# A two-layer diffusion backbone on one core: the first mixer's projection as three products of split operands, and weight splits ahead of every norm

## The reference, cut to what matters

```
def rmsnorm(x, g):
    x32 = x.astype(F32)
    y = x32 * lax.rsqrt(jnp.mean(x32 * x32, axis=-1, keepdims=True) + EPS)
    return y.astype(x.dtype) * g
def modulate(x, shift, scale):
    return x * (1 + scale) + shift
...
        a_lat = modulate(rmsnorm(h_lat, norm1_g[l]), sh1, sc1)
        a_ctx = modulate(rmsnorm(h_ctx, norm1_g[l]), sh1c, sc1c)
...
    hy_l, q_l, k_l, v_l = split(a_lat @ w_in)
    hy_c, q_c, k_c, v_c = split(a_ctx @ w_in)
```

## Time and profile before

| | us |
|---|---|
| median of 3 runs | 3494.87 |
| lowest and highest run | 3494.84, 3497.16 |
| the profiled execution | 3494.55 |
| its span, first to last instruction | 3492.7 |

### The profile page before, as it was taken

One profiled execution on the slowest core, in us unless ns is written; L12 is line 12 of the kernel. 1 busy time (PEld: TensorE's weight loads), 2 busy tenths in 40 slices (PEclk: granted clock), 3 DMA queues, 4 the chain that ended last, 5 costly groups with the idle time before them and its releaser, 6 DMA issues.

```text
span 3492.7 us, 46282 instructions
## 1 busy us (share of the span) xinstructions
PE 3290.8 (94%) x18808; PEld 2753.9 (79%) x18808; DVE 1976.6 (57%) x3318; ACT 1209.3 (35%) x1846; POOL 20.0 (1%) x41
## 2 busy tenths in 40 slices
PE   7898979999999999999999999898679999999998
PEld 3355548888888888888888887687569999999997
DVE  3125631899765566344444443434857988756665
ACT  1210422333333333333333332424334444444444
POOL 0000000000000000000000000000000000000000
PEclk9998899999999999999999999899799999999999
DMA  5330022555667666665656553222045777788884
GB/s 195 127 126 0 1 91 73 139 144 143 192 215 243 226 212 205 221 224 193 193 193 193 193 193 100 91 79 79 1 134 170 211 226 247 247 271 263 268 265 150
DMA packets 232411, 587.81 MB, mean 168 GB/s; under 512 B 20791, under 2 KB 103816, under 8 KB 228552
## 3 DMA queue, kind: packets, MB, share of 16 engines
q1 hardware_dynamic: 227088, 528.57, 48.2%
q0 software_dynamic: 4208, 53.27, 3.9%
q10 hardware_dynamic: 904, 3.01, 0.3%
HBM read 483.06 MB, written 101.71 MB: 167 GB/s over the span
## 4 chain that ended last, share of the span: by engine, by line
PE 86%; DVE 10%; ACT 2%; issue 1%; DMA 1%; POOL 0%; SPq 0%; ACTq 0%; DVEq 0%; POOLq 0%
PE ps L504 36%; PE ps L790 31%; PE ps L686 7%; PE ps L742 5%; PE ps L704 2%; PE ps L549 1%; DVE w_lo L1545 1%; PE ps L580 1%; DVE arena L1462 1%; PE ps L647 1%; PE ps L573 1%; PE ps L722 1%; DVE arena L1456 1%; PE ps L859 1%; PE ps L655 0%
## 5 line engine op out<-in xcount | busy, mean ns | idle before, releaser
L1545 DVE TENSOR_TENSOR w_lo<-wring,w_hi 128x1024 fp32r<-128x1024 f32 x512 | 626.0, 1223 | 687.0 <-ACT w_hi L1076 685.0
L504 PE MATMUL ps<-a_hi,w_hi 128*128 128x512 f32 (+1 forms) x2048 | 701.7, 343 | 8.5 <-DVE w_lo L1545 4.4
L790 PE MATMUL ps<-act_hi,w_hi 128*128 128x512 f32 (+1 forms) x2048 | 697.6, 341 | 4.4 <-DVE act_lo L1576 4.4
L504 PE MATMUL ps<-a_hi,w_lo 128*128 128x512 f32 (+1 forms) x2048 | 690.3, 337 | 0.0
L504 PE MATMUL ps<-a_lo_q,w_hi 128*128 128x512 f32 (+1 forms) x2048 | 689.6, 337 | 0.0
L790 PE MATMUL ps<-act_lo,w_hi 128*128 128x512 f32 (+1 forms) x2048 | 688.1, 336 | 0.0
L790 PE MATMUL ps<-act_hi,w_lo 128*128 128x512 f32 (+1 forms) x2048 | 687.6, 336 | 0.0
L1076 ACT CAST w_hi<-wring 128x1024 fp32r<-128x1024 f32 x512 | 533.6, 1043 | 226.8 <-PE ps L790 226.8
L504 PEld LDWEIGHTS ps<-a_hi,w_hi 128*128 128x128 f32 x2048 | 389.6, 190 | 60.9 <-issue 11.5
L790 PEld LDWEIGHTS ps<-act_hi,w_hi 128*128 128x128 f32 x2048 | 387.8, 189 | 51.7 <-issue 4.8
L504 PEld LDWEIGHTS ps<-a_hi,w_lo 128*128 128x128 f32 x2048 | 389.6, 190 | 41.6
(11 more groups left out here) (230 smaller groups left out, 3320.5 us busy)
## 6 DMA issues: line engine op xcount, KB each, us to landing
wring<-in_u SPq DMA_DIRECT2D x256, 512.0 KB, 4.1
wring<-in_v SPq DMA_DIRECT2D x256, 512.0 KB, 3.9
gates<-arena POOLq DMA_DIRECT2D x24, 2048.0 KB, 8.4
acts<-arena SPq DMA_DIRECT2D x128, 256.0 KB, 4.6
arena<-acts SPq DMA_DIRECT2D x128, 256.0 KB, 3.4
arena<-gates SPq DMA_DIRECT2D x16, 2048.0 KB, 11.3
late_ring<-in_ada SPq DMA_DIRECT2D x28, 1024.0 KB, 6.2
wring<-in_ada SPq DMA_DIRECT2D x40, 512.0 KB, 6.8
```

What stands on the lines that cost most here:

```text
L504: ins = pe.matmul(o, l, r, start=n == 0, stop=n == len(pairs) - 1, **kw)
L790: ins = pe.matmul(value_sum(l, c), w, x, start=m == 0 and n == 0 and (l == 0 or c % 2 == 0), stop=m == NKEY - 1 and n == 2, skip_group_che ...
L1545: tt(WLO[:, k % 4].rearrange("p k n -> p (k n)"), wring[:, n % RING * TILE:(n % RING + 1) * TILE], WHI[:, k % 4].rearrange("p k n -> p (k ...
```

## The change

The first projection becomes a split product like the others (entry `ab` of `SPLIT`, ring of two; its high activations are in two pieces, `AB_HI`). The values tile comes out transposed like the rest into `VV`, and PE turns it with four transposes behind `rope`. For all four norms, DVE splits the first weight tiles before it takes the norm's sum, `ring` of them instead of `ring - 1`, and interleaves the low parts with the chunks; PE runs the first `ring` tiles chunk by chunk beside each other, one output bank for each. `ada` counts on a semaphore of its own, `rows_used`, `w_used` starts at the output projection, and `key_numbers` on DVE moves behind `attention`, since `AB_HI` covers its place.

```diff
@@ tables
+        AB_HI = [over(f"ab_hi{n}", at, 4 * T)[:, :].rearrange("p (k t) -> p k t", k=4) for n, at in enumerate((31872, 18432))]
+        VV = arena[:, 33920:34432]
+        ab_parts = weight_parts("ab", 20480, 22528, 2)
+        SPLIT = {"ab": (None, N_ABIN, 0, 0, T, 2, ab_parts, A_LO_Q),
@@ SP, load
-                wait(sp, S["w_used"], n - RING + 1)
+                m = n - RING
+                if m >= AT_ABOUT:
+                    sp.wait_ge(S["w_used"], used(m))
+                elif m in AB_TILE:
+                    sp.wait_ge(S["ab_split"], AB_TILE[m] + 1)
+                elif m >= 0:
+                    sp.wait_ge(S["rows_used"], ADA_GROUP[m] + 1)
@@ PE
             def ab_in():
-                pe.wait_ge(S["a_ready"], KD)
+                if ada_leads(0):
+                    ada(FIRST_GROUPS)
+                first_tiles("ab", lambda j: ps[:, j, :], T, lambda j: None)
                 for j in range(N_ABIN):
-                    n = at_abin(j)
-                    if ada_leads(j):
-                        ada(FIRST_GROUPS + j)
-                    wait(pe, S["ab_taken"], j - 3)
...
+                    if j >= 2:
+                        if ada_leads(j):
+                            ada(FIRST_GROUPS + j)
+                        wait(pe, S["ab_taken"], j - 3)
+                        product("ab", j, ps[:, j % 4, :], T)
...
@@ PE, end of rope
+                for t in range(TT):
+                    ins = pe.transpose(ps[:, 6, t * P:(t + 1) * P], VV[:, t * P:(t + 1) * P], ident[:, :])
+                ins.then_inc(S["vt_ready"], 1)
@@ PE
+            def first_tiles(name, o, width, ready):
+
+                n0, _, _, k, _, ring, _, _ = SPLIT[name]
+                for c in range(KD):
+                    pe.wait_ge(S["a_parts_ready"], KD * k + c + 1)
+                    for j in range(ring):
+                        if c == 0:
+                            ready(j)
+                            split_done(name, j)
+                        product_part(name, j, c, o(j), width)
@@ PE, queries; hg_in likewise with two tiles
-                for j in range(N_WQ):
-                    wait(pe, S["wq_taken"], N_WQ * l + j - 3 if j >= 4 else 0)
+                first_tiles(f"wq{l}", lambda j: ps[:, j, 0:width], width, lambda j: None)
+                for j in range(4, N_WQ):
+                    pe.wait_ge(S["wq_taken"], N_WQ * l + j - 3)
@@ ACT
             def first_weights(name):
-                for j in range(SPLIT[name][5] - 1):
+                for j in range(SPLIT[name][5]):
                     weight_high(name, j)
@@ ACT, ab_in; queries and hg_in get the same "if j >= 1"
-                    act.wait_ge(S["w_used"], at_abin(j) + 1)
+                    if j >= 1:
+                        weight_high("ab", j + 1)
+                    act.wait_ge(S["product_ready"], j + 1)
@@ ACT, program
             act.wait_ge(S["x_in"], 16)
+            first_weights("ab")
             norm(0, T, 2)
             ab_in()
             hyena()
+            values_turned()
             attention()
@@ DVE
             def first_parts(name):
 
                 _, _, _, k, width, ring, _, a_lo = SPLIT[name]
-                for j in range(ring - 1):
+                for j in range(ring):
                     weight_low(name, j)
-                for c in range(KD):
-                    dve.wait_ge(S["a_hi_ready"], KD * (k - 1) + c + 1)
...
+                norm_sum(k, width)
+                for c in range(KD + 2):
+                    if c < KD:
+                        norm_part(k, c, width)
+                    if c >= 2:
+                        a_low(k, c - 2, width, a_lo)
@@ DVE, short_conv
-                for j in range(12):
+                for j in range(N_ABIN - 2):
+                    weight_low("ab", j + 2)
+                    if j >= 12:
+                        continue
                     dve.wait_ge(S["cv_mid"], j + 1)
```

More of the change, by code:

```diff
@@ L88, with used @@
 ADA_AT = [AT_ADA + 2 * g for g in range(FIRST_GROUPS)] + [at_ada_ab(j) for j in range(AB_GROUPS)]
+AB_TILE = {at_abin(j): j for j in range(N_ABIN)}
+ADA_GROUP = {n + x: g for g, n in enumerate(ADA_AT) for x in range(2)}
+def used(n):
+    return n - AT_ABOUT + 1
 HG_SPLIT = 24
@@ L558, in ada @@
                 r = ADA_AT[g] % RING
-                rows(g, W[:, r:r + 2], "w_used")
+                rows(g, W[:, r:r + 2], "rows_used")
             def late(j):
@@ L675, in attention, with split_done, product_part @@
                         values(u - 2)
+            def split_done(name, j):
+                if name == "ab":
+                    pe.wait_ge(S["ab_split"], j + 1)
+                else:
+                    pe.wait_ge(S["w_used"], used(SPLIT[name][0] + j))
+            def product_part(name, j, c, o, width):
+                n0, count, m0, k, _, ring, (w_hi, w_lo), a_lo = SPLIT[name]
+                for n, (w, x) in enumerate(parts(w_hi[:, j % ring, c, :], w_lo[:, j % ring, c, :],
+                                                 high_part(k, c, width), a_lo[:, c, 0:width])):
+                    ins = pe.matmul(o, w, x, start=c == 0 and n == 0, stop=c == KD - 1 and n == 2)
+                if c == KD - 1:
+                    ins.then_inc(S["product_ready"], 1)
+            def first_tiles(name, o, width, ready):
[7 more added lines that the diff above has]
+                        product_part(name, j, c, o(j), width)
             def product(name, j, o, width):
-                n0, count, m0, k, _, ring, (w_hi, w_lo), a_lo = SPLIT[name]
-                pe.wait_ge(S["w_used"], n0 + j + 1)
+                split_done(name, j)
                 for c in range(KD):
[L682 to L687, removed]
+                    product_part(name, j, c, o, width)
             def mixed(l, c):
@@ L794, in hg_in @@
             def hg_in():
-                for j in range(N_HGIN):
+                first_tiles("hg", lambda j: ps[:, j, 0:SEQ], SEQ, lambda j: None)
+                for j in range(2, N_HGIN):
                     n = AT_HGIN + j
@@ L958, in norm @@
                     ins.then_inc(S["a_ready"], 1)
-                    if 1 <= k < 4:
+                    if k < 4:
                         act.wait_ge(S["a_ready"], KD * k + c + 1)
-                        copy(A_HI[:, c, 0:width], A[:, c, 0:width]).then_inc(S["a_hi_ready"], 1)
+                        copy(high_part(k, c, width), A[:, c, 0:width]).then_inc(S["a_hi_ready"], 1)
             def weight_high(name, j):
@@ L1315, in gains_of, with norm_sum @@
                         ALU.add, ALU.mult).then_inc(S["mods_ready"], 1)
-            def norm(k, width):
+            def norm_sum(k, width):
                 dve.wait_ge(S["norm_summed"], k + 1)
@@ L1604, in forget @@
                 first_parts("hg")
-                for j in range(1, 9):
+                for j in range(2, 9):
                     weight_low("hg", j)
@@ L1764, in _ @@
             peer_residual(0)
-            norm(2, T)
             forget()
```

85 lines of the change are left out of this document (46 added, 39 removed).

## The result

| us | before | the change |
|---|---|---|
| median (4 runs each) | 3495.22 | 3461.14 |
| lowest and highest run | 3494.84, 3497.16 | 3456.80, 3461.74 |
| the profiled execution, its span | 3494.55, 3492.7 | 3461.03, 3459.2 |

The ratio is 0.9899, with a 95% interval from 0.9884 to 0.9914 (it is taken from all the runs; the two medians alone give 0.9902). So the change is faster by 1%, clear of the noise: by 34.1 us where 40.5 were forecast, and inside the range. The mean granted clock is 0.973, as before. PE is busy for 3272.0 us instead of 3290.8, so on balance some 19 us of the difference are shorter work on PE, and the rest is waiting that has gone. The chain is still PE's, which answers the earlier trace rows.

A forecast was written before the change was run, and what follows sets the result against it. PE's products, and the places where PE stands still, were taken as the bound. Savings of 10.0 + 23.3 + 3.9 + 1.1 + 2.2 = 40.5 us gave a span of 3452.2 and a time of 3454.4 us; range 3449 to 3463.

The forecast's parts named there:

- their measured price: First projection: a split product takes 0.227 us at clock 1.00; a tile of 24 takes 5.44 us, unsplit 7.06.
- 3 us of cover: First projection, behind an odd tile: weight parts have 3 us to spare; each us beyond would cost one per tile.

The follow-up runs named there:

- ab_only: The change's first projection with its norm 0, norms 1 to 3 in the old order of the kernel before; 3459.4 us, ratio 0.9902 to before.
- norms_only: The kernel before with the change's new order at norms 1 to 3 alone; 3493.55 us, ratio 0.9999 to before.
- casts_behind_tiles: casts_behind with chunks 4 to 7 of the first four tiles run tile by tile at norms 1 and 3; 3445.81 us, ratio 0.9857.
- squares_split: squares_early with the casts and low parts of the first weights halved around the root; 3428.9 us, ratio 0.9811 to before.
- change_again: The changed kernel once more, unedited, beside later variants; 3461.46 us, ratio 0.9905 to before.
- one_by_one: The change with a norm's first tiles run one after the other on PE, not side by side; 3464.55 us, ratio 0.9923 to before.
- casts_behind: The change with ACT's casts of the first weight tiles moved behind the squares at norms 1 to 3; 3449.31 us, ratio 0.987 to before.
- busy_ahead: The change plus 24 unread matmuls on PE ahead of the sums of norms 1 and 3; 3451.97 us, ratio 0.9884 to before.
- hg_busy: The change plus ten small unread matmuls on PE behind the first two tiles of norm 2; 3452.75 us, ratio 0.9885 to before.
- squares_early: casts_behind_tiles with each square right behind its residual chunk and norm 2's sum in bank 0; 3431.31 us, ratio 0.9825 to before.
- pad3: The change plus three small ACT copies ahead of each cast from tile 3 on in the first projection; 3459.82 us, ratio 0.99 to before.
- pad8: The change plus eight small ACT copies ahead of each cast from tile 3 on in the first projection; 3489.6 us, ratio 0.9986 to before.

## What to carry to other kernels

Where PE is the bound, count passes first: three short products in place of one long took the stretch down by what their measured price said, and the order of the work around it needed only to keep 3 us of cover. What an instruction costs ahead of a norm isn't always its own duration: if PE stands idle meanwhile, the products that follow can pay again in clock, so put such work behind the step that feeds PE, or give PE something to do. And a reordering that wins 5 us behind a norm wins little (2.3 us at norm 1, nothing that the medians can tell) when the work that it moves ahead stands on the same path.

## What the hardware showed that I had not expected

**A stretch with two lengths.** From Hyena's transposes to the output projection's residual the work is the same in all these kernels, but it mostly took one of two lengths: 228.4 to 229.3 us in before, the change, ab_only, norms_only, casts_behind_tiles, squares_split and change_again, and 223.5 to 224.7 in one_by_one, casts_behind, busy_ahead, hg_busy and squares_early (pad3 226.9, pad8 230.8). It arises at the start of attention. The changed kernel, then hg_busy, which is identical up to there:

```profile
300.00:320.00 20.00, 17.31 (x44) 9.52 (x44) 12.44 (x35) 7.77 (x20) 0.00 (x0) 0.50 0.00 0
320.00:336.00 16.00, 15.24 (x54) 8.25 (x52) 10.09 (x30) 6.29 (x19) 0.00 (x0) 0.69 0.00 1
```

```profile
300.00:320.00 20.00, 16.63 (x53) 8.96 (x53) 14.20 (x39) 8.14 (x21) 0.00 (x0) 0.66 0.00 0
320.00:336.00 16.00, 14.14 (x74) 8.11 (x73) 12.86 (x42) 9.37 (x28) 0.00 (x0) 1.00 0.01 1
```

In the one PE stays at 0.50 for 20 us and more, in the other it rises sooner and does 74 products in the next 16 us instead of 54. PE and the other two engines feed each other there, so a low clock may keep itself alive for a while; no run tests that. The two kernels issue the same instructions in the same order up to there (the edit is at norm 2), so that order doesn't select it. What does stays open; each length was seen in one profiled execution of a kernel only, and the runs of single kernels spread by 5 us and more (3456.8 to 3461.7 for the change, 3439.5 to 3452.4 for casts_behind_tiles). For a measurement of this kernel it means that a median of four runs tells two kernels apart only above some 5 us.

**The fall behind partly busy work.** At norm 2 PE stood for 2.5 us behind chunks that had kept it busy for 62% of the time (3.20 of 5.20), and the next tile ran at 0.60; at norm 1 it stood for longer and the sums began at 0.50. Both cost something on top of the standing itself: 1.5 and 2.7 us, by hg_busy and busy_ahead. How much of the low level the work gets was not the same each time. The sums of norm 2 took 9.67 and 9.37 us with no cast ahead of them (casts_behind, casts_behind_tiles), 8.56 and 8.58 with one (before, ab_only), and with two 10.0 in six kernels, but 9.68 in hg_busy and 8.55 in one_by_one. At norm 1 the two kernels with four casts and short sums, 8.5 for 9.9, are also two with the short attention stretch. What the two have in common stays open.
